# Norm rates as exp(-ln(v)/2) on ScalarE, and another order of transfers and work in the head, in a three-layer fp32 kernel on one core

## What is computed

```
def rmsnorm(x, g):
    xf = x.astype(jnp.float32)
    y = xf * lax.rsqrt(jnp.mean(xf * xf, axis=-1, keepdims=True) + EPS)
    return (y * g.astype(jnp.float32)).astype(x.dtype)

def adaln_in(x, g, m, i):
    return rmsnorm(x, g) * (1 + m[:, i, 1][:, None]) + m[:, i, 0][:, None]

def swiglu(h, w1, w3, w2):
    return (jax.nn.silu(h @ w1) * (h @ w3)) @ w2

    cond = jax.nn.silu(c)
    m = (cond @ w_mod[l] + b_mod[l]).reshape(bsz, 3, 3, D_MODEL)   # per layer
    x = x + 0.5 * m[:, 0, 2][:, None] * swiglu(adaln_in(x, norm_g[l, 0], m, 0), ...)
```

## Time and profile before

| | |
|---|---|
| runs of the kernel | 1513.23, 1517.08, 1518.96 us; median 1517.08 |
| the profiled execution | 1512.4 us, its span 1510.3 us |
| mean granted TensorE clock | 0.992 |
| PE busy | 96% of the span |
| DVE (VectorE) busy | 74% |
| ACT (ScalarE) busy | 47% |
| chain that ended last | PE 85%, DVE 9%, ACT 3%, issue 2%, DMA 1% |
| DMA | 309.33 MB, mean 205 GB/s |

### The profile page before, as it was taken

How to read it: one execution, slowest core, us unless ns; L and a number is a source line. 1 busy time by engine, 2 the same in 40 slices (tenths; PEclk the granted TensorE clock), 3 DMA queues, 4 the chain that set the end, 5 groups by cost and what they waited for, 6 DMA issues and landing times.

```text
span 1510.3 us, 26953 instructions
## 1 busy us (share of the span) xinstructions
PE 1446.3 (96%) x11188; PEld 1365.6 (90%) x11188; DVE 1122.8 (74%) x1849; ACT 706.3 (47%) x1126; POOL 23.2 (2%) x24
## 2 busy tenths in 40 slices
PE   4999999999999999999999999999999889899998
PEld 4999999789999999999988689999996669899998
DVE  6888988877787879878768667555586776677776
ACT  2433436444433453334364434434465765564543
POOL 0000000000000000001000000000000030000000
PEclk9999999999999999999999999999999899999999
DMA  9986956146868467576632145555421304345542
GB/s 390 415 357 245 363 216 260 57 159 250 317 257 328 182 271 294 211 289 280 234 128 99 56 168 195 212 201 202 181 85 63 138 23 143 123 168 181 197 172 81
DMA packets 32330, 309.33 MB, mean 205 GB/s; under 512 B 3497, under 2 KB 5801, under 8 KB 7505
## 3 DMA queue, kind: packets, MB, share of 16 engines
q1 hardware_dynamic: 32208, 307.60, 52.9%
HBM read 306.53 MB, written 1.06 MB: 204 GB/s over the span
## 4 chain that ended last, share of the span: by engine, by line
PE 85%; DVE 9%; ACT 3%; issue 2%; DMA 1%; SPq 0%; DVEq 0%; ACTq 0%
PE bank L650 13%; PE bank L654 13%; PE bank L651 13%; PE bank L806 13%; PE bank L720 6%; PE bank L718 6%; PE bank L725 6%; PE bank L620 3%; DVE WL L1707 2%; PE bank L666 1%; PE bank L886 1%; DMA X<-in_x 1%; PE bank L875 1%; PE bank L611 1%; PE bank L672 1%
## 5 line engine op out<-in xcount | busy, mean ns | idle before, releaser
L1707 DVE TENSOR_TENSOR WL<-ring,WH 128x1024 fp32r<-128x1024 f32 x420 | 502.2, 1221 | 51.2 <-ACT WH L1195 49.0
L1195 ACT ACTIVATE WH<-ring 128x1024 fp32r<-128x1024 f32 x420 | 429.7, 1054 | 132.1 <-PE bank L806 51.0
L650 PE MATMUL bank<-XH,WH 128*128 128x256 f32 x1680 | 409.3, 282 | 1.4 <-ACT WH L1195 1.4
L651 PE MATMUL bank<-XL,WH 128*128 128x256 f32 x1680 | 407.7, 281 | 0.0
L650 PEld LDWEIGHTS bank<-XH,WH 128*128 128x128 f32 x1680 | 316.1, 188 | 7.1 <-issue 5.5
L651 PEld LDWEIGHTS bank<-XL,WH 128*128 128x128 f32 x1680 | 316.2, 188 | 0.5 <-issue 0.5
L654 PE MATMUL bank<-XH,WL 128*128 128x256 f32 x1680 | 233.9, 282 | 1.0 <-DVE WL L1707 1.0
L654 PEld LDWEIGHTS bank<-XH,WL 128*128 128x128 f32 x1680 | 213.9, 188 | 1.2 <-DVE WL L1707 1.2
L1269 ACT ACTIVATE SG<-bank 128x256 f32<-128x256 f32 x88 | 33.8, 384 | 370.0 <-PE bank L654 359.0
L718 PE MATMUL bank<-GH,WH 128*128 128x256 f32 x840 | 202.6, 279 | 0.7 <-ACT WH L1195 0.7
L720 PE MATMUL bank<-GL,WH 128*128 128x256 f32 x840 | 202.5, 279 | 0.0
(11 more groups left out here) (311 smaller groups left out, 1719.6 us busy)
## 6 DMA issues: line engine op xcount, KB each, us to landing
ring<-in_stream SPq DMA_DIRECT2D x133, 1536.0 KB, 6.6
scr<-in_stream SPq DMA_DIRECT2D x15, 1536.0 KB, 10.9
PR<-in_stream SPq DMA_DIRECT2D x15, 1536.0 KB, 8.2
att<-in_stream SPq DMA_DIRECT2D x15, 1536.0 KB, 10.9
ring<-in_stream SPq DMA_DIRECT2D x8, 1024.0 KB, 5.0
ring<-in_stream SPq DMA_DIRECT2D x11, 512.0 KB, 3.6
kf_mix<-in_stream SPq DMA_DIRECT2D x2, 1536.0 KB, 16.7
con<-in_consts SPq DMA_DIRECT2D x1, 2000.0 KB, 19.6
```

What stands on the lines that cost most here:

```text
L650: pe.matmul(o, part(WH, u, k), XH[:, k, :], start=(k == 0), stop=False)
L651: pe.matmul(o, part(WH, u, k), XL[:, k, :], start=False, stop=False)
L1195: act.activation(part_all(WH, u), raw(u), ACT.Copy).then_inc(*mark("high", u))
L1707: dve.tensor_tensor(part_all(WL, u), raw(u), part_all(WH, u).bitcast(F32), ALU.subtract)\
```

## The change

On ScalarE every `Sqrt` of a norm or a head's norm becomes `Ln` with the same bias and scale, followed (with a wait on its own semaphore) by an `Exp` of scale -0.5 over the same tile; VectorE's reciprocals go. Banks are free for PE at the log. The Sqrt of the filter's norm and of the recurrence stay as they are. The dummy activations that brought in the Sqrt table become a direct load of the table with both functions, and those that switched between Exp and Sqrt around attentions go. Five keep-warms replace twelve in all six places. In the head: c first on the queue, the ones behind mod item 1, x behind mod item 3, of mod item 5 only row 0, its two gate rows behind ("ffn", 0, 0); VectorE scales first, then splits WL, then does the lows, then the gate rows; the first units of FFN 0 run in another order (`head_up`). SP's wait for mod_read 5 stays, and mod_read 5 is now marked behind the gate rows. The keep-warms of the head keep their numbers; the last waits for `ada_in`.

```diff
+            sp.dma_start(cond[:, :], c_d.partition_broadcast(P)).then_inc(*mark("c_in", n=16))
             sp.dma_start(par[:, :], param_d).then_inc(*mark("par_in", n=16))
-            sp.dma_start(cond[:, :], c_d.partition_broadcast(P)).then_inc(*mark("c_in", n=16))
-            sp.dma_start(con[:, 0:2 * P], const_d[:, 0:2 * P]).then_inc(*mark("ones_in", n=16))
...
+                    n = D if i == HEAD_MODS - 1 else n
+                    sp.dma_start(mod_slots[k][:, 0:n], stream[ITEM_AT[name], :, 0:n]).then_inc(sig.sem(f"mod_landed{k}"), 16)
...
+                if name == ("ffn", 0, 0):
+                    i = HEAD_MODS - 1
+                    sp.dma_start(mod_slots[i][:, D:ITEM], stream[ITEM_AT["mod", i], :, D:ITEM]).then_inc(*mark("gate_rows_in", n=16))
                 if name == ("mod", 1):
+                    sp.dma_start(con[:, 0:2 * P], const_d[:, 0:2 * P]).then_inc(*mark("ones_in", n=16))
+                if name == ("mod", 3):
                     sp.dma_start(X, x_d).then_inc(*mark("x_in", n=16))
...
+                def head_up(b, units):
+
+                    for k in range(KD):
+                        pe.wait_ge(*at("norm_high", key, k))
+                        for a, u in units:
+                            if k == 0:
+                                pe.wait_ge(*at("high", u))
+                            pe.matmul(b[:, a * S:(a + 1) * S], part(WH, u, k), XH[:, k, :], start=(a == 0 and k == 0), stop=False,
+                                      skip_group_check=True)
+                    for a, u in units:
+                        pe.wait_ge(*at(*low_of(u)))
+                        for k in range(KD):
+                            pe.matmul(b[:, a * S:(a + 1) * S], part(WL, u, k), XH[:, k, :], start=False, stop=False,
+                                      skip_group_check=True)
+                    for k in range(KD):
+                        pe.wait_ge(*at(*normed(key, k)))
...
-                                keep_warm(12)
+                                keep_warm(5)
...
-                pe.wait_ge(*at("mod_read", i))
+                pe.wait_ge(*(at("mod_read", i) if i < HEAD_MODS - 1 else at("ada_in", 0, 0)))
                 keep_warm(14 if i < HEAD_MODS - 1 else 8)
...
+            def load_rates():
+
+                act.preload_act_table_set("natural_log_exp_and_others")
...
-                act.activation(norm_rstd(k), norm_stat(k), ACT.Sqrt, bias=prm("eps"), scale=1.0 / width)\
-                    .then_inc(*mark("stat_root", k))
+                act.activation(norm_rstd(k), norm_stat(k), ACT.Ln, bias=prm("eps"), scale=1.0 / width)\
+                    .then_inc(*mark("stat_log", k))
+                act.wait_ge(*at("stat_log", k))
+                act.activation(norm_rstd(k), norm_rstd(k), ACT.Exp, scale=-0.5).then_inc(*mark("stat_root", k))
...
                 squares(k, waits)
-                load_table(ACT.Sqrt)
+                load_rates()
                 root(k)
...
                 dve.wait_ge(*at("stat_root", k))
-                link(dve.reciprocal(norm_rstd(k), norm_rstd(k)))
...
-            def head_inverse(k):
-                o = HEADS[k]["base"]
-                dve.wait_ge(*at("head_root", k))
-                dve.reciprocal(hstd[o:o + 16, :], hstd[o:o + 16, :]).then_inc(*mark("head_rstd", k))
...
-            for i in range(HEAD_MODS):
+            for i in range(HEAD_MODS - 1):
                 for r in range(MOD_ROWS):
                     mod_row(i, r)
-                if i == 2:
-                    norm_root(("sub", 0, 0))
+            mod_row(HEAD_MODS - 1, 0)
+            scale_rates(0, 0)
+            norm_root(("sub", 0, 0))
             for l in range(2):
                 if l == 0:
-                    split_to(up_units(0, 0)[1])
-                    norm_parts_of(("sub", 0, 0))
+                    norm_parts_of(("sub", 0, 0), lambda: split_to(up_units(0, 0)[1]))
+                    dve.wait_ge(*at("gate_rows_in"))
+                    for r in range(1, MOD_ROWS):
+                        mod_row(HEAD_MODS - 1, r)
```

More of the change, by code:

```diff
@@ L674, in first_up @@
                         last.then_inc(*mark("w1_used" if a == 0 else "ffn_up", f, 0))
+                def head_up(b, units):
[13 more added lines that the diff above has]
+                        pe.wait_ge(*at(*normed(key, k)))
+                        for a, u in units:
+                            last = pe.matmul(b[:, a * S:(a + 1) * S], part(WH, u, k), XL[:, k, :], start=False,
+                                             stop=(k == KD - 1), skip_group_check=True)
+                            if k == KD - 1:
+                                last.then_inc(*mark("w1_used" if a == 0 else "ffn_up", f, 0))
                 def down(c):
@@ L1161, in _ @@
             win2_and_attention()
[L1162 removed]
+            take(6, "stat_log", "mla")
             norm_sum("mla")
@@ L1433, in head_root @@
                 a = PARAM["eps"][0]
-                act.activation(hstd[o:o + 16, :], bank[HEADS[k].get("stat", 6)][o:o + 16, 0:S], ACT.Sqrt, bias=par[o:o + 16, a:a + 1],
-                               scale=1.0 / HEADS[k]["width"]).then_inc(*mark("head_root", k))
+                act.activation(hstd[o:o + 16, :], bank[HEADS[k].get("stat", 6)][o:o + 16, 0:S], ACT.Ln, bias=par[o:o + 16, a:a + 1],
+                               scale=1.0 / HEADS[k]["width"]).then_inc(*mark("head_log", k))
+                act.wait_ge(*at("head_log", k))
+                act.activation(hstd[o:o + 16, :], hstd[o:o + 16, :], ACT.Exp, scale=-0.5).then_inc(*mark("head_rstd", k))
             def attention(a, between=lambda h: None):
@@ L1502, in _ @@
             act.wait_ge(*at("stat_sum", "mem"))
-            act.activation(norm_rstd("mem"), norm_stat("mem"), ACT.Sqrt, bias=prm("eps"), scale=1.0 / D).then_inc(*mark("stat_root", "mem"))
+            act.activation(norm_rstd("mem"), norm_stat("mem"), ACT.Ln, bias=prm("eps"), scale=1.0 / D).then_inc(*mark("stat_log", "mem"))
+            act.wait_ge(*at("stat_log", "mem"))
+            act.activation(norm_rstd("mem"), norm_rstd("mem"), ACT.Exp, scale=-0.5).then_inc(*mark("stat_root", "mem"))
             def gates(d):
@@ L1561, in _ @@
                 if j == 11:
+                    load_rates()
                     head_root("mk")
                     act.wait_ge(*at("q_var"))
-                    act.activation(rates[:, 0:16], rates[:, 0:16], ACT.Sqrt).then_inc(*mark("q_root"))
+                    act.activation(rates[:, 0:16], rates[:, 0:16], ACT.Ln).then_inc(*mark("q_log"))
+                    act.wait_ge(*at("q_log"))
+                    act.activation(rates[:, 0:16], rates[:, 0:16], ACT.Exp, scale=-0.5).then_inc(*mark("q_root"))
                 evict(j)
@@ L1641, in _ @@
             act.wait_ge(*at("e_stat"))
-            act.activation(rates[:, 0:8], bank[6][:, 0:8], ACT.Sqrt, bias=prm("eps"), scale=1.0 / P).then_inc(*mark("e_root"))
-            load_table(ACT.Exp)
+            act.activation(rates[:, 0:8], bank[6][:, 0:8], ACT.Ln, bias=prm("eps"), scale=1.0 / P).then_inc(*mark("e_log"))
+            act.wait_ge(*at("e_log"))
+            act.activation(rates[:, 0:8], rates[:, 0:8], ACT.Exp, scale=-0.5).then_inc(*mark("e_root"))
             attention("e")
@@ L2291, in _ @@
             norm_lows("mla")
-            resid("wout2", None, lambda m: head_inverse("memk") if m == 2 else None)
+            resid("wout2", None)
             norm("memx", lambda: split_to(first_unit("wmq") + 1))
```

46 lines of the change are left out of this document (21 added, 25 removed).

## The result

The changed kernel took 1500.03 us (median of 5 runs, 1499.38 to 1507.37) against 1518.49 of the kernel before (5 runs): a ratio of 0.9883, interval 0.986 to 0.9907. Forecast were 1507.7 and at least 1501.5. The profiled execution of the changed kernel is its slowest run: 1507.37, span 1505.5, mean clock 0.986; the other four lie at 1499.4 to 1500.2 with 0.992 or 0.993. One later execution of the kernel before took 2032.65 us at a mean clock of 0.651, unlike any other here, and enters no number of this document.

The account below looks back on a forecast made before the run. PE was taken as the bound, busy 1446 of 1510 us. Terms -6.65 - 0.1 - 1.65 - 0.7 - 1.3 + 1.0 = -9.4 took 1512.4 to 1503.0; adding 4.7 for the median gave 1507.7, range 1501.5 to 1516.5.

Parts of the forecast that it names:

- (d): Heads' four reciprocals, seven attention table loads and small roots q and e: hidden beside PE or DVE, costed at nothing.
- (e): Head: new transfer and modulation order; PE's own order makes the first unit's Silu later, 48.6 against 47.67: +1.0 us.
- (b): Norms with other work behind the sums: sub 1,1 -0.1 us, attn2 -1.65 from fewer keep-warms, memx -0.7.
- (a): Rates by Ln and Exp without the reciprocal: 1.33 us gained at each of five norms, -6.65 in all.
- (c): Norms lru and mla: wout2 starts 0.45 later, but mla's scaling and lows come 1.3 earlier for the waiting splits: -1.3 us.
- R2: Rival: DVE's and ACT's freed time reaches PE at heads and attentions, 3.2 us, giving 1504.5; chance 0.11.
- R1: Rival: head sums run at full rate, 3.62 instead of 6.38, so the head gives -1.8; 1504.9 in all; chance 0.12.
- The queues: Head: SP's later wait for mod_read 5 leaves the queue dry a microsecond at most; costed at nothing, 1 to 2 us if starved.
- R3: Rival: PE's clock falls behind the shortened keep-warms at six places, 1.9 us each, giving 1519.1; chance 0.08.

Follow-up runs that it names:

- 5: The changed kernel with 12 keep-warms instead of 5 at all six places; median 1503.58 us, 1504.1 at like clock.
- 6: The changed kernel with two reciprocals put back on VectorE ahead of scaling at norms sub 1,1 and ckv each; median 1507.33 us, 1507.6 at like clock.
- 3: The changed kernel without its head part, keeping the new rates, loads and five keep-warms; median 1503.63 us, ratio 0.9902 to the kernel before.
- 8: The changed kernel with 3 keep-warms four times in the head, gate rows multiplied later, no keep-warm ahead of attn2; median 1504.56 us, 1500.0 at like clock.
- 11: The changed kernel with 3 keep-warms four times in the head, none ahead of attn2, win2's unit 10 behind the query sums; median 1495.88 us.
- 12: Repeat: the changed kernel with short head keep-warms, none ahead of attn2, and win2's unit 10 behind the query sums; median 1494.64 us.
- 10: The changed kernel with win2's projection unit 10 moved behind the query sums of heads 0 to 3; median 1499.04 us, 1499.7 at like clock.

## Why the prediction was wrong

The forecast was 7.7 us too high. Its base, the 4.7 between profiled execution and median, holds 3.2 of them, and its steps hold 4.5: 1.7 in (d), where a reciprocal was never priced, 1.3 in (e), 0.8 in (b) at sub 1,1 and 0.5 at memx, 0.2 in small ones. The steps that were priced came true in kind; what failed is the base, the path that was left out, and the cover that I saw at sub 1,1.

**Step (a), right.** Five norms at 1.33; measured 1.33 to 1.40, 6.8 in all for 6.65. The keep-warm cut adds nothing there (5).

**Step (b), wrong at sub 1,1, right at attn2.** I took the spectra's end as 759.69 + 3.60 = 763.29 and found the projection's start behind it, so PE looked busy throughout. But a matmul's end is modelled and overlaps its successor's start: the row that begins at 763.41 names no wait,
```profile
763.41 0.36 PE L806 MATMUL bank<-XH,WH 128*128 128x256 f32 x1
```
yet the eight spectra were 3.72 apart from it and are 3.03 apart from it now (758.23 to 761.26). PE had stood still for 0.7, hidden in the overlap, and with XH ahead of it 0.2 more came in the unit behind, by my reading because its first matmuls no longer wait for parts of XH. In 6 the wait comes back as 2.31. The 1.33 on XH's path was right; the cover was not. At memx likewise: 0.7 forecast and 0.77 measured up to the first matmul, 0.4 more in the unit. attn2's 1.65 was 1.55, and 5 shows that it is the keep-warms'.

**Step (c), right.** The +0.45, and -1.88 at the splits' wait: -1.4 for -1.3.

**Step (d), wrong by omission; the largest miss of the steps.** The earlier trace rows count twelve reciprocals into the norms' tile. Parts (a) to (c) and the head name eleven; ckv's was never followed (nor mem's, which writes elsewhere). I wrote that the freed time of heads would stay beside PE, which is so at a, c and mk, and R2 looked for it in attention. It came out at neither but at ScalarE's wait for the lows of norm mem, 18 us behind the reciprocal: -1.7, and 6 shows the path by lengthening it. The rest of R2 is out: the heads' reciprocals and the seven loads lie in the table's "small rest", -0.2. PE's waits in the profile before had the row, below larger ones; I read only the largest:
```profile
PE bank L1092 <- ACT scr L1509: 2.5, 1, 2.5
```

**Step (e), mechanism right, size wrong by 1.3.** X landed at 23.65 instead of 24.45 (-0.8), the keep-warms began 6.1 behind the sums' start instead of 6.4 (-0.3) and took 11.1 for 11.4 (-0.3), and the unit 6.0 for 5.8 (+0.2). R1 is out, since the sums took 0.39 each. What the sum hid, 3 took apart: the new rates give the old head 1.8, and the new order takes 1.5 of it. The queues cost nothing, as said; in 8, with the slot held until 48.0, they cost 4.7.

**The rest is the base.** The steps missed 4.5 us. The other 3.2 are in "the median is 4.7 above the profiled execution". That carried the scatter of before over to after as a constant. It is not one: it depends on how many executions belong to the group with the lower clock. The 14 profiles bear this out. The four at a mean clock of 0.992 or 0.993 (before, 6, 11, 12) have at most 7 us at half clock between 1143 and 1190, the ten at 0.984 to 0.988 have 17 to 31. Of before the lower group has 53 of 70 executions, of the changed kernel's first five one. 1512.4 - 13.9 is 1498.5; the median is 1.5 above it, not 4.7. That part was chance as far as the runs show: with three of the five in the lower group the median would have been near 1505 and within the range.

**R3.** Its place was wrong: no norm reads 0.50. The risk to the clock is real and cost more than R3's price in single executions, where nothing of the change stands. The Trainium skill ("TensorE: Matmul & The Clock Gate", Part 1) has the clock follow how busy the array has been recently. If "busy" is read as the profile's column, the trace does not agree: at the norms PE stood still for up to 1.34 and the clock stayed, and between 1160 and 1170 both profiles of before say 9.31 of 10.00, one at 1.00 and one at 0.50. The same section of the Trainium skill notes, of the first matmuls of a kernel, that the count of slow ones differs from run to run. The two profiles of before show such a difference in mid-kernel, 10.9 us between 1157 and 1170.

**Still open:** why the changed kernel had fewer such executions than before (4 of 11 against 53 of 70), and whether the changed kernel or an order like that of 10 does it. The head part alone, whose stage near 1150 is that of before, had 5 of 12 in the group with the higher clock. Why the clock falls in this work in one execution and not in another is open altogether.

## What to carry to other kernels

When an operation is replaced everywhere, take its count from the row of the group and follow every one of them to who waits for it, to the end of the engine's unbroken run of work and not just to the next matmul; and where PE rows overlap, judge a wait by the distance of starts, not by modelled ends. Ask for the clock and time of each execution before a median is carried over: where an execution can lose 8 us at one place, a median moves with the shares of the groups, and changes are to be compared within one group. Look at keep-warms last but look at them: in this head and ahead of attn2 they were themselves the path, and cutting them was worth 5 to 6 us at like clock, where the whole change gave 13.

## What the runs showed of the hardware

- For one kernel and its data, the granted clock over the small products of the memory attention (keys of 64 columns, sums of one and of 16 columns) differs between executions, at full and at half level with PE's busy column at 93 to 100%; a pair of profiles of the kernel before comes 10.9 us apart within 13 us of work. In eight of the 11 kernels here the time follows the mean clock with 1.0 to 1.3 us for 0.001.
- Exp from and to SBUF took 0.42 for 128x256 and followed the Ln that it depends on, on the same engine, after 0.04; no table load came between them.
- 5 keep-warms (10 instructions) and 0.91 to 1.34 us of idle time behind them left the granted clock at 1.00 at all five norms that have nothing else there.
- Longer waits of PE went either way: 2.45 us ahead of 1143.98 in the profile before left the clock at 1.00; 2.83 us ahead of 1139.07 in 6 and 4.32 us ahead of 56.21 in 8 had 3.4 us at 0.50 at their end, from 1139.34 and from 55.70. The wait of 4.54 to 4.60 us near 1200, ahead of an attention's L899 (L928 in most kernels), overlaps a half-clock stretch in all 14 profiles.
